# A decoder trunk on one core: one wait fewer in the first weight loads, and a copy placed behind a weight split

## The reference, cut to what matters

```python
x = (1, 4096, 1024) float32
h = rms_norm(x, ln_g)
proj = einsum('bsd,de->bse', h, w_in)          # 1024 x 2816, split in nine groups of columns
u_pool, g_pool, c_a, c_b, g_conv, q, k, v, g_attn = split(proj)
y_pool = pool_mixer(u_pool) ; y_conv = conv_module(c_a, c_b)
y_attn = sliding_window_attention(q, k, v, sinks)   # 8 query heads, 2 kv heads of 64, window 128
y = concat([y_pool * silu(g_pool), y_conv * silu(g_conv), y_attn * silu(g_attn)])
x = x + einsum('bse,ed->bsd', y, w_out)
out = rms_norm(x, final_g)
```

## Time and profile before

| | |
|---|---|
| median of 3 runs | 1418.95 us (1417.42 to 1420.05) |
| time of the profiled execution | 1420.05 us |
| its span (first to last instruction) | 1418.3 us |
| what lies around the span | 1.75 us |
| PE busy | 98% of the span |
| DVE, ACT, POOL busy | 84%, 39%, 27% |
| granted TensorE clock | full over all of the 40 slices |

### The profile page before, as it was taken

One profiled execution on the slowest core, in us unless ns is written; L12 is line 12 of the kernel. 1 busy time (PEld: TensorE's weight loads), 2 busy tenths in 40 slices (PEclk: granted clock), 3 DMA queues, 4 the chain that ended last, 5 costly groups with the idle time before them and its releaser, 6 DMA issues.

```text
span 1418.3 us, 20098 instructions
## 1 busy us (share of the span) xinstructions
PE 1392.4 (98%) x6814; PEld 1138.8 (80%) x6814; DVE 1188.9 (84%) x2455; ACT 553.0 (39%) x1428; POOL 384.5 (27%) x592
## 2 busy tenths in 40 slices
PE   6999999999999999999999999999999999999997
PEld 4878787787878787878888888888888888888886
DVE  5787878787878776677999998989999998898886
ACT  5666565555565554422122112121132243333332
POOL 5122323324232333120001011010110355555551
PEclk9999999999999999999999999999999999999999
DMA  9616071525343324535123033030327575555531
GB/s 214 202 29 252 17 241 62 200 104 171 125 163 133 134 119 117 210 61 206 35 114 134 15 149 133 15 133 34 145 97 275 237 241 175 179 175 162 163 108 75
DMA packets 89366, 196.91 MB, mean 139 GB/s; under 512 B 13904, under 2 KB 55248, under 8 KB 81616
## 3 DMA queue, kind: packets, MB, share of 16 engines
q1 hardware_dynamic: 65616, 172.48, 34.2%
q10 hardware_dynamic: 23680, 23.60, 6.4%
HBM read 114.27 MB, written 81.79 MB: 138 GB/s over the span
## 4 chain that ended last, share of the span: by engine, by line
PE 83%; DVE 12%; SPq 1%; ACT 1%; DMA 1%; issue 1%; ACTq 0%; POOLq 0%; POOL 0%; DVEq 0%
PE wide L345 11%; PE wide L347 11%; PE wide L346 11%; PE pair L1145 10%; PE pair L1149 10%; PE pair L1146 9%; DVE m_tail L1896 5%; PE pair L1127 3%; PE wide L1163 2%; PE wide L1164 2%; PE turn L347 2%; PE turn L345 2%; PE turn L346 2%; PE pair L347 2%; PE pair L345 2%; PE pair L346 2%
## 5 line engine op out<-in xcount | busy, mean ns | idle before, releaser
L1896 DVE SCALAR_TENSOR_TENSOR m_tail<-m_tail,m_taps 128x512 f32<-128x512 f32 x480 | 338.4, 750 | 4.6
L1145 PE MATMUL pair<-xT,w_hi 128*128 128x512 f32 x632 | 252.9, 400 | 6.3 <-DVE w_lo L409 4.6
L1149 PE MATMUL pair<-xT,w_hi 128*128 128x512 f32 x632 | 248.1, 393 | 0.0
L1146 PE MATMUL pair<-xT,w_lo 128*128 128x512 f32 x632 | 247.6, 392 | 0.0
L107 POOL TENSOR_TENSOR pool_carrier<-pool_carrier 128x1 f32<-128x1 f32 x77 | 27.0, 351 | 707.4 <-DVE m_meanvar L1905 400.1
L1649 POOL TENSOR_TENSOR operand_sums<-m_y 128x512 f32<-128x512 f32 x75 | 102.1, 1362 | 167.7 <-PE wide L347 116.6
L1145 PEld LDWEIGHTS pair<-xT,w_hi 128*128 128x128 f32 x632 | 119.3, 189 | 33.7 <-DVE w_lo L409 5.0
L1149 PEld LDWEIGHTS pair<-xT,w_hi 128*128 128x128 f32 x632 | 119.0, 188 | 29.5 <-DVE xT L338 2.6
L1146 PEld LDWEIGHTS pair<-xT,w_lo 128*128 128x128 f32 x632 | 119.4, 189 | 21.7
L774 POOL TENSOR_SCALAR a_rows<-a_rows,a_inv 128x128 f32<-128x128 f32 x256 | 109.1, 446 | 76.5 <-DVE a_inv L974 76.5
L345 PE MATMUL wide<-x_first,w_hi 128*128 128x512 f32 x320 | 125.5, 392 | 0.0
(11 more groups left out here) (261 smaller groups left out, 2925.7 us busy)
## 6 DMA issues: line engine op xcount, KB each, us to landing
xT_scratch<-xT SPq DMA_DIRECT2D x16, 2048.0 KB, 8.5
x_first<-xT_scratch SPq DMA_DIRECT2D x16, 1024.0 KB, 7.9
xT<-xT_scratch SPq DMA_DIRECT2D x16, 1024.0 KB, 9.1
combo_scratch<-stage SPq DMA_DIRECT2D x28, 512.0 KB, 4.1
m_y<-y_scratch ACTq DMA_DIRECT2D x14, 1024.0 KB, 6.7
xs<-in_x_dram SPq DMA_DIRECT2D x20, 512.0 KB, 8.7
y_scratch<-y_out SPq DMA_DIRECT2D x8, 1024.0 KB, 4.2
y_scratch<-y_out SPq DMA_DIRECT2D x16, 512.0 KB, 2.8
```

The costliest lines, as they stand in the source:

```text
L1145: nc.tensor.matmul(out, w_hi, st.hi[:, kk, :], start=(kk == 0), stop=False)
L1146: nc.tensor.matmul(out, w_lo, st.hi[:, kk, :], start=False, stop=False)
L1149: last = nc.tensor.matmul(out, w_hi, st.lo[:, kk, :], start=False, stop=(kk == KT - 1))
L1896: nc.vector.scalar_tensor_tensor(out=conv[:, i, :], in0=h[:, i, j:j + TB], scalar=taps[:, i, j:j + 1], in1=conv[:, i, :], op0=ALU.mult, op ...
```

## The change

There are two edits. SP no longer waits for chunk K before it issues the loads of chunks Q, Q+1 and G. And in ACT's program for a block, the split of combo slot 4 moves from behind the copy of v to the place ahead of it, next to slot 3 (and ahead of `split_hi` of a chunk that only the last block has, where there are no combos).

```diff
@@ -665,7 +665,6 @@
     def sync(sp):
         st.load_first(sp)
         w.load(sp, CHUNK_K, (0, 1))
-        sp.wait_ge(w.loaded[CHUNK_K], 16 * SUB)
         w.load(sp, CHUNK_Q, (0, 1))
         w.load(sp, CHUNK_Q + 1)
         w.load(sp, CHUNK_G)
@@ -893,14 +892,12 @@
             q_hi(n, 3)
             if not first and not final:
                 st.scale(act, n + 1, 2)
-            for s in combos.of_block(n, (3,)):
+            for s in combos.of_block(n, (3, 4)):
                 combos.split_hi(act, s)
             if final:
                 w.split_hi(act, CHUNK_CA)
             act.wait_ge(st.squared, SUB + st.HALF * (n if final else n + 1))
             copy_out(n, slot("v"), vT)
-            for s in combos.of_block(n, (4,)):
-                combos.split_hi(act, s)
             if not first and not final:
                 st.scale(act, n + 1, 3)
             act.wait_ge(v_turned, n + 1)
```

## The result

| | median us | runs | profiled execution | its span |
|---|---|---|---|---|
| before | 1419.98 | 5, 1417.42 to 1420.75 | 1420.05 | 1418.3 |
| after | 1427.87 | 5, 1426.31 to 1431.62 | 1427.81 | 1426.1 |

The ratio is 1.0062, with an interval of 1.005 to 1.0075: slower by 7.9 us in the medians and by 7.8 in the two profiled spans. The ratio is taken over 17 executions of after, whose median is 1428.47 us; that is why it comes to 8.8 us and not to 7.9. The forecast was 1421.5 and the range ended at 1424.0, so the time lies outside it.

A forecast was written before the change was run, and what follows sets the result against it. PE, busy 98% of the span, was taken as the bound. The moved split's 2.5 us plus 0 for the removed wait gave 1422.5 from the profiled 1420.05, or 1421.5 on the median's scale; range 1418.8 to 1424.0.

The forecast's parts named there:

- The first edit's 0: Opening: without SP's wait K lands 0.8 us later from shared DMA, costing PE 0; ends 0 and 1.8.
- The cover by POOL: Opening: DVE's low part of K stands still until POOL's instruction ends, so K up to 1.07 us later costs nothing.
- The choke rival: Opening: SP held at a full line also holds ACT's issue of K; PE 4 us later, 1425.5; chance 0.08.
- K late as well: Opening: the slower shared DMA rate lands K 2.1 us later, costing 1.3 us; sum 3.8, time 1422.8; chance 0.24.
- Not slower: Blocks: slack before turn_v or PE's later products take the holds back; 1419.0 to 1419.5; chance 0.12.
- faster: Early Q and early DVE work help PE, at most 1.66 us, with no holds in blocks 1 to 5: 1417.3; chance 0.06.
- 2.5 us: Blocks 1 to 5: later copies of v hold turn_v by 1.09, 0.06, 0.45, 0 and 0.91 us; ends 1.9 and 3.1.
- a fresh start of PE: Blocks: PE restarting after each of three holds may add as much as the slack takes off, at most 0.3 us.
- no relief of DVE would shorten a block: Blocks: DVE's last low part comes up to about 0.8 us sooner, but block 6, without this work, is no shorter.

The follow-up runs named there:

- e1: Kernel before with only SP's wait for chunk K removed, ACT's block order unchanged; 1424.89 us, ratio 1.0042.
- e2: Kernel before with only the split of slot 4 moved ahead of the copy of v, SP's wait kept; 1423.06 us, ratio 1.0026.
- e4: Kernel before with SP's wait for chunk K moved behind the loads of Q and Q+1, ahead of G; 1426.13 us, ratio 1.0049.
- e8: Kernel before with the splits of slots 3 and 4 both behind the copy of v on ACT; 1423.07 us, ratio 1.0024.
- e7: Kernel before with ACT issuing its loads of K after two squares, not three, SP's wait kept; 1418.95 us, ratio 0.9995.
- e10: Kernel before without SP's wait for K, and SP loading the lower halves of Q+1 and G before their upper halves; 1423.31 us, ratio 1.0029.
- e5: Kernel before without SP's wait for K, and ACT issuing its loads of K ahead of all squares; 1421.76 us, ratio 1.0014.

## Why the prediction was wrong, point by point

**The first edit's 0 is the step that failed.** It was put so: "What changes is company", and "When both queues are full they share evenly", with K 0.8 or 2.1 us later as the outcome of one or the other rate. That is what the queues do once both are moving; it left out that ACT's loads do not begin to share at once. PE's first projection started at 23.54, where the prediction had called itself wrong from 18.8 on. K's high part started 5.73 us later, 4.8 of it before ACT's first packet moved (14.3 against 9.5), 0.9 from the shared rate. So the second half of the step came out about right (0.8 had been taken), and the first half was missing from the sum. That the second half fits is in part luck: in e1, with the same edit and the loads on the same half of the partitions for longer, K's high part starts 7.3 us behind the first packet against 5.4 before, 1.9 more. The trace of before had the number that told it: K's two parts on ACT were issued at 7.57 and moved only from 9.5, behind 512 packets of SP's. The prediction read the stretch from 9.5 on and did not ask why it began there.

The Trainium skill (DMA: Bandwidth & Descriptors, "Queues, rings and completion order") says that each engine takes turns, packet by packet, between the queues that it has work for. The 98 and 96 of 19 to 20 us agree. The rule alone would not have foretold the 6.5 us before, in which q10 moved nothing; whether ACT's packets had reached the engines by then no run shows.

**The cover by POOL did not matter.** A delay of up to 1.07 us was to be free. K came later than all that, and met POOL again at another place: the low part took 1.78 at 21.71, started into POOL's select that ran from 21.31 to 22.40. The one run that allows a look at the rule itself bears it out: in e2 K came 1.6 us later than before, its low part took 1.23 and not 2.15, and PE started only 0.7 later.

**The choke rival** (0.08, 1425.5) had the size of the opening right, PE 4 us later against 5.4, and the wrong cause: e4 shows the whole delay while SP holds no issue back for its last 5 us. "No row shows the two queues in that state" was an argument for a wide range; the prediction took it as one for a small chance, and left this rival out of the range.

**"K late as well"** (0.24, 1422.8) had the right sign and 1.3 us where the runs have 5.4 to 6.6. **"Not slower"** and **"faster"** fall: PE took none of the holds back, and Q came later, not sooner.

**The second edit was right in mechanism and a little small.** Against 2.5 us the blocks show 2.96 in after and 3.5 in e2; the forecast blocks were 76.4, 75.3, 75.7, 75.3, 76.2 and 75.28, and after has 76.41, 75.55, 75.83, 75.29, 76.30 and 75.35. In after the copy of v starts later in blocks 1, 2, 3 and 5 by 1.20, 0.27, 0.55 and 1.02 us, 3.04 in all, where 1.09, 0.06, 0.45 and 0.91 had been taken. The mis-sized term is the distance from the split to the copy behind it: 0.54 was read from a split followed by a scaling, and it is 0.65 to 0.66 in front of the copy (137.46 to 138.12 in block 1). That is 0.11 for each held block. In block 2 the plain split began 0.1 later in the block than the store's landing had it, since it stood behind the split of slot 3, and the copy stood 0.65 behind it and not 0.54. These four blocks are 1.12, 0.28, 0.54 and 1.01 us longer than before, so the later copy explains them, and no price of its own for a fresh start of PE shows. That no relief of DVE would shorten a block was right; what was said with it, that DVE's load does not set a block's length, is true for less work and not for work that comes later, as e8 shows.

**The rest.** Opening 5.36 with 1.03 less up to block 1, blocks 2.96, end 0.5 make the 7.8. That the -1.03 and the 0.5 belong to the change is not shown; both lie in the spread over the kernels.

## What to carry to other kernels

A wait in front of a bulk load can be what keeps another queue's urgent load quick: before it is removed, count the packets that will stand issued when the urgent load is issued, take most of them as ahead of it, and move the urgent load in front of them if it can be. An earlier issue that passes none of them gains nothing (e7). In block 1 of after the copy of v started 1.20 us later, since it stood behind a split that was not ready: an instruction that is moved ahead of one on the critical path must be ready there, not only short; look at what its operands wait for. And where the trace doesn't show a resource in the state that the change creates, its bound belongs in the range, whatever the chance one would give to a particular story.

## What the runs showed of the hardware

- A DMA issued on ACT's queue began to move only after most of the packets that SP had issued before it: 1.9, 4.4 and 6.5 us behind its issue for about 512, 1024 and 1740 packets of 1 KB, and 4.7 us (e7) for 512 of them with 222 packets of x, of 4 KB each, still ahead. What is issued on SP afterwards made no difference (e4 against after). While both queues had work, they then had equal shares (98 and 96).
- With two queues on partitions 64 to 127 the DMA engines moved 200 packets per us, as with one; with one queue on 0 to 63 and the other on 64 to 127 it was 343 to 360 in e10 from 16 to 19 us, and only 216 and 252 in before and e5 near 10 us.
- POOL's select and DVE's subtraction with two inputs exclude each other in both directions. In e7 DVE was first by 0.02 us, and now POOL's took twice as long:

```profile
17.28 1.23 DVE L409 TENSOR_TENSOR w_lo<-a_rows,w_hi 128x1024 fp32r<-128x1024 f32 x1 [3.48 <-ACT w_hi L404]
17.30 2.16 POOL L746 TENSOR_SCALAR_AFFINE_SELECT a_gate<-a_gate 128x1024 f32<-128x1024 f32 x1
```

Where it is first, such a select takes 1.09. The kernel before has the same pair of instructions in the other order, by 0.02 us too, and DVE's took 2.15. Each time the second takes longer by 0.9 to 1.1 us, about as long as the first is running.
